# A routed-expert stage whose loop is skewed by one matrix, with another ending

## The reference, cut to what matters

```python
logits = t @ router_w + router_b            # t = rmsnorm(x) * norm_ffn_w, (320, 1024)
vals, idx = lax.top_k(logits, 4)            # 4 of 32 experts for each row
gates = jax.nn.softmax(vals, axis=-1)
for e in range(32):
    a = jnp.minimum(t @ w_gate[e] + b_gate[e], 7.0)
    u = jnp.clip(t @ w_up[e] + b_up[e], -7.0, 7.0)
    hid = (u + 1.0) * a * jax.nn.sigmoid(1.702 * a)
    y = y + combine[:, e:e + 1] * (hid @ w_down[e] + b_down[e])
x = x + y
y_prompt, y_sample = rmsnorm(x, final_norm_w)
```

## Time and profile before

| | |
|---|---|
| median of three executions | 1128.1 us (1128.0 to 1129.16) |
| the profiled execution, its own time | 1130.27 us |
| its span, first to last instruction | 1128.4 us |
| mean granted clock of TensorE | 0.994 |
| TensorE busy | 1103.0 us, 98% |
| VectorE / ScalarE / GpSimd busy | 394.5 / 162.7 / 18.2 us |
| DMA | 431.67 MB, mean 383 GB/s |
| chain that ended last | TensorE 79%, DMA 19%, VectorE 1% |

### The profile page before, as it was taken

The page is one execution under the profiler, slowest core; times in us unless marked ns, Lnnn a source line. Parts: engine busy times, 40 slices in busy tenths (PEclk is TensorE's granted clock), DMA queues, the critical chain, the costliest instruction groups (busy, mean ns, idle before and its releaser), DMA issues.

```text
span 1128.4 us, 15518 instructions
## 1 busy us (share of the span) xinstructions
PE 1103.0 (98%) x6341; PEld 454.0 (40%) x6341; DVE 394.5 (35%) x703; ACT 162.7 (14%) x284; POOL 18.2 (2%) x45
## 2 busy tenths in 40 slices
PE   8999999999999999999999999999999999999997
PEld 5657754433333333333333333333333333333333
DVE  4165385433333333333333333333333333233233
ACT  3100124211111111111111111111111111111102
POOL 0002000000000000000000000000000000000000
PEclk9999999999999999999999999999999999999997
DMA  9970247999999999999999999999999999999991
GB/s 323 333 227 22 129 159 298 396 428 427 436 428 430 432 432 433 429 432 433 432 430 432 432 432 432 431 432 432 433 431 431 432 433 429 429 429 428 427 423 63
DMA packets 41442, 431.67 MB, mean 383 GB/s; under 512 B 3809, under 2 KB 23069, under 8 KB 26431
## 3 DMA queue, kind: packets, MB, share of 16 engines
q1 hardware_dynamic: 40592, 430.38, 91.3%
q10 hardware_dynamic: 815, 0.82, 0.2%
HBM read 427.48 MB, written 3.71 MB: 382 GB/s over the span
## 4 chain that ended last, share of the span: by engine, by line
PE 79%; DMA 19%; DVE 1%; ACT 0%; issue 0%; SPq 0%; DVEq 0%
PE ps L1428 47%; DMA ring<-in_w_gate 15%; PE ps L1135 9%; PE ps L1402 5%; DMA ring<-in_w_up 4%; PE ps L1254 3%; PE ps L1319 3%; PE ps L1411 2%; PE ps L1322 1%; PE ps L1390 1%; PE ps L1471 1%; PE ps L1125 1%; PE ps L1384 1%; DMA x<-in_x_sample 0%; PE ps L1511 0%; PE ps L1513 0%
## 5 line engine op out<-in xcount | busy, mean ns | idle before, releaser
L1428 PE MATMUL ps<-ring,RT 128*64 128x512 f32 x3072 | 689.8, 594 | 11.7 <-DMA ring<-in_w_gate 10.3
L1428 PEld LDWEIGHTS ps<-ring,RT 128*64 128x64 f32 x3072 | 210.5, 137 | 410.3 <-issue 381.7
L985 DVE SCALAR_TENSOR_TENSOR x<-ps,gates,x 128x1024 f32<-128x1024 f32 (+1 forms) x93 | 102.9, 1106 | 127.6 <-PE ps L1402 126.5
L1135 PE MATMUL ps<-R,ring 128*128 128x320 f32 x384 | 107.5, 436 | 0.3 <-issue 0.3
L991 DVE TENSOR_TENSOR RT<-ps,R 128x512 f32<-128x512 f32 x32 | 22.1, 692 | 228.9 <-ACT R L632 228.9
L1135 PEld LDWEIGHTS ps<-R,ring 128*128 128x128 f32 x384 | 71.8, 190 | 31.2 <-issue 1.8
L1402 PE MATMUL ps<-R 64*128 64x512 bf16 x558 | 76.8, 381 | 0.0
L1025 DVE TENSOR_SCALAR RT<-ps 128x512 f32<-128x512 f32 x32 | 22.1, 692 | 143.1 <-PE ps L1428 143.1
L624 ACT ACTIVATE RT<-RT 128x512 f32<-128x512 f32 x32 | 20.2, 630 | 300.1 <-DVE RT L1019 300.1
L1402 PEld LDWEIGHTS ps<-R 64*128 64x128 bf16 x558 | 20.8, 98 | 86.0 <-issue 50.3
L603 ACT ACTIVATE RT<-ps 128x512 f32<-128x512 f32 x33 | 19.7, 597 | 237.1 <-PE ps L1322 237.1
(11 more groups left out here) (226 smaller groups left out, 559.2 us busy)
## 6 DMA issues: line engine op xcount, KB each, us to landing
ring<-in_w_gate SPq DMA_DIRECT2D x26, 4096.0 KB, 32.5
ring<-in_w_up SPq DMA_DIRECT2D x25, 4096.0 KB, 32.0
ring<-in_w_down SPq DMA_DIRECT2D x25, 4096.0 KB, 32.8
ring<-in_w_up SPq DMA_DIRECT2D x14, 2048.0 KB, 39.0
ring<-in_w_down SPq DMA_DIRECT2D x13, 2048.0 KB, 39.8
ring<-in_w_gate SPq DMA_DIRECT2D x12, 2048.0 KB, 40.8
ring<-in_w_in SPq DMA_DIRECT2D x14, 1024.0 KB, 12.7
ring<-in_w_out SPq DMA_DIRECT2D x4, 1024.0 KB, 10.0
```

The source lines that it names most:

```text
L985: STT(xb[b], rows, gates[:, par, b:b + 1], xb[b], ALU.mult, ALU.add).then_inc(accDone, 1)
L1135: ins = MM(ps[:, n % 2, 0:NT], slot_k(L, 256)[:, k, 128 * half:128 * half + 128], hT[:, k, :], start=(k == 0), stop=(k == KT - 1))
L1428: ins = MM(shape(ps[64 * half:64 * half + 64, bank, :]), lhs(k), cols(w, half), start=False, stop=(k == KT - 1))
```

## The change

1. **The loop is skewed.** TensorE now works gate and up of expert `j`, then down of expert `j - 1`. The matrices are loaded and used in the order g0 u0 g1 u1 d0 g2 u2 d1 ... g31 u31 d30 d31. The scatter put into the gate product of expert `j` is that of `j - 2`. `turn_gates` and `turn` of the next expert are put into the down product, after blocks 1 and 3. The transposes of the hidden activations stand between the down product and the next gate product. There are five buffers each of `eh`, `PT` and `gates` in place of three; `hidT` gets a place of its own.
2. **The last expert's rows are scattered as float32**: one copy of the product to SBUF (`yLast`), one float32 copy of the one-hot matrix (`PTLast`), 6 matmuls, no split.
3. **The final norm's weight comes by a transfer** that repeats it over the partitions, into a ring buffer that is free by then.
4. **The branch on rounds is turned**: `if rounds < 2: ending; else: further rounds, ending`.

```diff
+    I_GATE, I_UP, I_DOWN = [0] + [3 * j - 1 for j in range(1, E)], [1] + [3 * j for j in range(1, E)], [3 * j + 4 for j in range(E - 1)] + [MATS - 1]
@@ further_rounds
-            with eng.If(rounds > 1):
+            with eng.If(rounds < 2):
+                ending()
+                eng.nop()
+            with eng.Else():
                 close_round(0)
...
-                eng.nop()
-            with eng.Else():
+                ending()
                 eng.nop()
@@ sync engine
+            def outputs():
+
+                sp.wait_ge(wUsed, 4 * NEXT + START)
+                sp.dma_start(fnw[0], A["final_norm_w"].partition_broadcast(128)).then_inc(fnwIn, 16)
+                for half in range(2):
+                    w = A["final_norm_w"][HALF * half:HALF * half + HALF]
+                    sp.dma_start(fnw[2][64 * half:64 * half + 64], w.partition_broadcast(64)).then_inc(fnwIn, 16)
...
@@ ScalarE, one expert
+                        sigmoid(e)
+                        keep_rows(m, before)
+                        keep_slots(m, before * 3, buf(j + 1))
...
                         act.activation(ysb[0], ps[:, 2, :], ACT.Copy).then_inc(yHigh, 1)
-                        act.wait_ge(yRest, e + 1 + START)
+                        keep_hidden(e)
+                        act.wait_ge(yRest, before + 1 + START)
                         act.activation(ysb[1], yrest, ACT.Copy).then_inc(yMid, 1)
...
+                act.activation(PTLast[:], PT[buf(E - 1)], ACT.Copy).then_inc(ptLastOut, 1)
+                act.wait_ge(wUsed, (r + 1) * (LPE * E) + START)
+                act.wait_ge(xgTOut, p0 + (E + 1) + START)
+                act.activation(yLast, ps[:, 2, :], ACT.Copy).then_inc(yHigh, 1)
@@ TensorE
+                def gate_up(e, m, j, it, between=()):
+
+                    pe.wait_ge(ehDone, m + 1 + START)
+                    pe.wait_ge(xgTOut, m + 1 + START)
+                    pe.wait_ge(aDone, e + START)
+                    product(0, half_c(xgT), I_GATE[j], it, buf(j), between)
+                    pe.wait_ge(uDone, e + START)
+                    product(1, half_c(xgT), I_UP[j], it, buf(j))
+                    gather(m + 1)
+
+                def down(e, j, it, between):
+
+                    pe.wait_ge(yRest, e + START)
+                    product(2, half_c(hidT), I_DOWN[j], it, buf(j), between, operand=(hidTOut, e + 1 + START))
+
+                gate_up(e0, p0, 0, 0)
+                turn_hidden(e0)
+                turn_gates(p0 + 1)
+                turn(p0 + 1)
                 def experts(it, these):
 
                     for j in these:
...
+                        gate_up(e, m, j, it, [lambda: None] + [lambda b=b: scatter(b, e2, m2, buf(j - 2)) for b in range(3)] if j > 1 else [])
+                        down(before, j - 1, it, [lambda: turn_gates(after), lambda: turn(after)])
+                        turn_hidden(e)
...
+                down(e0 + (E - 1), E - 1, 0, [lambda b=b: scatter(b, e0 + (E - 2), p0 + (E - 2), buf(E - 2)) for b in range(3)])
+                pe.wait_ge(ptLastOut, r + 1)
+                pe.wait_ge(yHigh, e0 + E + START)
...
+                        ins = MM(to, PTLast[64 * half:64 * half + 64, t0:t0 + n], yLast[64 * half:64 * half + 64, :],
+                                 start=True, stop=True)
...
-            for part, ready in enumerate((yHigh, yMid, yLow)):
-                pe.wait_ge(ready, E + START)
-                for b, (t0, n) in enumerate(TOK):
...
-            for k in range(D // 128):
-                row = ident[0:FN + 8, FN + k:FN + k + 1]
-                at = 128 * (k % 4)
-                MM(ps[:, 4 + k // 4, at:at + 128], row.broadcast_to([FN + 8, 128]), parRows[:], start=True, stop=True)
-                half = slice(64 * (k // 4), 64 * (k // 4) + 64)
-                ins = MM(ps[half, 2, at:at + 128], row.broadcast_to([FN + 8, 64]), parRows[:], start=True, stop=True)
-            ins.then_inc(fnwMM, 1)
```

More of the change, by code:

```diff
@@ L404, in _ @@
+            further_rounds(sp, all_loads, ending=outputs)
             sp.wait_ge(yOut, 64)
@@ new lines, in norms @@
+            def norms():
+                bring_table(ACT.Sqrt, 3)
+                for b in range(3):
+                    act.wait_ge(accDone, 3 * (E - 1) + b + 1 + START)
+                    if b:
+                        act.wait_ge(finSq, b)
+                    act.activation(junk2[:, 0:WIDE[b]], xb[b], ACT.Square, accum_out=st[:, b:b + 1]).then_inc(finSq, 1)
+                    if b < 2:
+                        act.wait_ge(finSq, b + 1)
+                        total = st[:, b:b + 1]
+                    else:
+                        act.wait_ge(finFoldMM, 1)
+                        total = ps[:, 5, 0:1]
+                    act.activation(st[:, 3 + b:4 + b], total, ACT.Sqrt, bias=epsT[:], scale=1.0 / D).then_inc(finRoot, 1)
@@ L640, in _, with close_round @@
+            def close_round(r):
+                act.wait_ge(accDone, (r + 1) * (3 * E) + START)
+                act.sem_inc(aloneA, 1)
             one_round(0)
             act.wait_ge(roundsDone, 1)
[L642 to L655 removed]
+            further_rounds(act, one_round, close_round, ending=norms)
@@ L1029, in experts @@
-                        dve.wait_ge(accDone, e * 3 + 3 + START)
-                        keep_gates(m, col, buf(j + 1))
-                        gathered(m)
-                        split_rows(e)
-                experts(0, range(FIRST))
+                        rows = (p0 + (it * PER_LOOP + (j - 2)), e0 + (it * PER_LOOP + (j - 2)), buf(j - 2)) if j > 1 else ()
+                        gate_up(e, m, col, j, r * (LPE * E) + it * (LPE * PER_LOOP), rows)
+                        split_rows(e0 + (it * PER_LOOP + (j - 1)))
@@ L1055, in _, with scales @@
-            for b in range(3):
-                dve.wait_ge(lastMM, b + 1)
-                rows = ps[:, LAST[b]:LAST[b] + 2, :].rearrange("p a n -> p (a n)") if b < 2 else ps[:, LAST[b], :]
-                STT(xb[b], rows, gates[:, buf(E - 1), b:b + 1], xb[b], ALU.mult, ALU.add).then_inc(moeDone, 1)
-            dve.wait_ge(moeDone, 3)
-            dve.wait_ge(fnwMM, 1)
-            for b in range(3):
-                final_scale(b)
+            def scales():
+                dve.wait_ge(fnwIn, 48)
+                for b in range(3):
+                    dve.wait_ge(finRoot, b + 1)
+                    dve.reciprocal(st[:, 6 + b:7 + b], st[:, 3 + b:4 + b]).then_inc(finScale, 1)
+                    dve.wait_ge(finScale, b + 1)
+                    STT(yout[:, b, 0:WIDE[b]], xb[b], st[:, 6 + b:7 + b], fnw[b], ALU.mult, ALU.mult).then_inc(finDone, 1)
@@ L1065, in _ @@
+            further_rounds(dve, one_round, rounds=rounds[0], ending=scales)
         @block.tensor
@@ L1461, in experts @@
-                        pe.wait_ge(xgTOut, m + START)
-                        pe.wait_ge(aDone, e + START)
-                        product(0, 0, half_c(xgT), e, it, j, [lambda: None] + [lambda b=b: scatter_before(b) for b in range(3)]
-                                if not isinstance(e, int) or e > 0 else [])
-                        pe.wait_ge(uDone, e + START)
-                        product(1, 1, half_c(xgT), e, it, j)
-                        gather(m)
-                        pe.wait_ge(hidDone, e + 1 + START)
@@ L1469, in experts @@
-                        pe.wait_ge(hidTOut, e + START)
-                        for c in range(4):
-                            ins = TR(ps[:, 4, 128 * c:128 * c + 128], fourth(hid, c), ident)
-                        ins.then_inc(hidTMM, 1)
-                        turn_gates(m)
-                        turn(m)
-                        pe.wait_ge(yRest, e + START)
-                        product(2, 2, half_c(hidT), e, it, j, operand=(hidTOut, e + 1 + START))
-                experts(0, range(FIRST))
+                        e, m = e0 + (it * PER_LOOP + j), p0 + (it * PER_LOOP + j)
```

265 lines of the change are left out of this document (134 added, 131 removed).

## The result

| | before | changed |
|---|---|---|
| median | 1128.63 us (four executions) | 1169.93 us (1168.71 to 1171.02, four) |
| ratio | | 1.0363, 95% interval 1.0345 to 1.0381 |
| the profiled execution, its span | 1130.27, 1128.4 us | 1171.02, 1169.2 us |
| mean granted clock of TensorE | 0.994 | 0.981 |

The forecast was 1122.3 us (range 1120.3 to 1126.2). The time is 47.6 us above it, on the other side, and beyond every rival.

What follows compares the result with a forecast made beforehand. The prediction took the weight transfer stream as the bound, TensorE close behind with 11.7 us of slack. A 7.8 us shorter ending and a 2.0 us later last product gave -5.8 us: 1122.3 us, range 1120.3 to 1126.2.

Steps and rivals of the forecast that it cites:

- every rival: Mild TensorE bound 1126.9 us (0.12), slower TensorE 1131.9 (0.08), visible end jump 1124.5 (0.09), serial float32 halves 1123.2 (0.09), free skew 1121.3.
- the stream has no hole to fill: Weight transfers during the expert loop: said to run full from 226 us on, at 427 to 436 GB/s.
- nothing of its own: Turned branch ahead of the ending: no separate gain counted, since VectorE's 2 us were hidden behind L1511.
- The ending, -7.8: From the last product's end to the first scale's reciprocal: 5.2 us rather than 13.0, so 7.8 us shorter.
- The float32 halves: Last expert's scatter: two row-tile halves taken to run together, 0.86 us a pair; if not, +0.9 us, chance 0.09.
- The jump at the end, taken 0, bound +2.5: Jump over further rounds, now after the ending: taken as hidden behind output transfers, at most one fetch, 2.5 us.
- a sign against it: Kernel's end: more than 4 us between the last issue of y_sample and the end would show the prediction wrong.
- The skew, +0.39 us an expert: TensorE's expert loop: three more layout changes an expert, 0.39 us, 12.1 us over 31 experts; bounds 0 and 0.54.
- T0 + 2.0: End of the last product: 2.0 us later than 1108.3, by TensorE's limit of 1110.3 against the stream's 1109.3.
- 0.13 each: TensorE's expert loop: each change of the array's layout was priced at 0.13 us.
- The sum: Whole kernel: -7.8 + 2.0 = -5.8 us, profiled execution 1124.5 us, median 2.2 us lower at 1122.3 us.

Runs made afterwards that it cites:

- run 7: Kernel before with only the final norm's weight brought by a transfer: 1125.68 us, ratio 0.9973.
- run 4: Kernel before with the norm's weight by a transfer and the branch on rounds turned on TensorE, VectorE and ScalarE: 1125.73 us, ratio 0.9968.
- run 1: Changed kernel with 100 unused semaphore increments strewn among TensorE's first projections, ahead of its loop: 1125.47 us, ratio 0.9962.
- run 9: Changed kernel with 32 unused semaphore increments ahead of TensorE's loop: 1125.8 us (one run).
- run 5: Changed kernel with 40 unused semaphore increments ahead of TensorE's loop: 1125.1 us (one run).
- run 12: run 6 with `turn_gates` and `turn` in one place of the down product rather than two: 1123.8 us, ratio 0.9959 to the kernel before.
- run 6: Changed kernel with 100 semaphore increments ahead of TensorE's loop, TensorE's and SyncE's jump over further rounds again ahead of the ending: 1123.85 us, ratio 0.9953.

## Why the prediction was wrong

**The step that failed** is one that the prediction did not take: it priced the loop body's instructions and said that "the stream has no hole to fill", counted "nothing of its own" for the turned branch, and weighed fetched code only at the branch on rounds, once, with a bound of 2.5 us. It never asked what the loop's own return costs once the code ahead of it changes length. The row that would have asked stood in the page of before: 22 packets of 16 KB for a program of which 6341 matmuls and as many weight loads were executed, some 50 packets' worth, means that the loop was not fetched again in five returns, and that this is a state which can be lost. Its price was in no row of before; but a single fetch after a branch cost VectorE 2.53 us, so even one in each of five returns is 12.7 us, twice the forecast gain. The section of the Trainium skill that the prediction cites for the branch on rounds holds the room of 2048 instructions too, a few lines away, and a loop of 1614 with the next block comes near it; the prediction used only the sentence that it was looking for. No rival held this; the range ended 44 us short. The runs showed in its place five returns of 9.1 to 9.5 us more each, 44.5 us of the time, which a shift of the code takes away.

By its own terms:

- **The ending, -7.8.** Right: 7.6 (16.7 less 9.1), seen in the changed kernel itself. The transfer brought 4.4 of it (run 7, forecast 4.5). The float32 halves do run beside each other: first sum at T0 + 1.9.
- **The jump at the end, taken 0, bound +2.5.** Mis-sized. From the first issue of y_sample to the end it was 3.4 us before, and 5.6 in the changed kernel, 5.2 in run 4, 4.95 in run 1, 4.7 and 4.5 in runs 9 and 5: 1.1 to 2.2 more. From the last issue to the end of the changed kernel it is 4.5 us (1164.7 to 1169.2), which the prediction had named as a sign against it. The rule of the Trainium skill that the prediction cites for it, that the jump is paid, agrees with these figures. What the prediction missed is that instruction packets run beside the outputs' transfers, which then take longer (3.8 us for 2.7), so the outputs are no cover. Turned in TensorE, VectorE and ScalarE, the branch gave nothing (run 4 against run 7).
- **The skew, +0.39 us an expert.** Right: 28.13 less 27.75 is 0.38, without a wait. That layouts cost 0.08 rather than 0.13 each in run 12 leaves some of the 0.38 to something else, or says that its changes are not all alike.
- **T0 + 2.0.** 1110.5, 1109.7, 1110.2, 1108.9 and 1109.4 in the shifted forms (forecast 1110.3 by TensorE, 1109.3 by the stream): right within 1.4, and nearer the stream's figure. In runs 5, 6, 9 and 12 the chain goes through the landing of the last up matrix, at 1083.3 to 1084.5 (forecast 1083.9), so the stream and not TensorE was the later one.
- **The sum.** The shifted kernel's profiled execution took 1126.44 us against 1124.5: 0.2 from T0, 0.2 from the scales, 1.5 from the end. Its median lies 3.2 above the forecast, since the forecast took 2.2 us off for the way from the profiled execution to the median, and here that was 1.0. The skew alone wasn't run; skew and float32 scatter together add nothing that can be told to the transfer and the branch (run 1 against run 4, 1125.5 and 1125.7).

## What to carry to other kernels

Before a change that alters the length of code ahead of or inside a hardware loop, read the queue of instruction packets: if there are far fewer packets than executed instructions divided by 256, the loop lives on code that is kept, and a shift of its place can end that (here 160 instructions did, and 32 brought it back); when a change loses time in equal pieces at each return, with "issue" as the releaser, shift the code by fillers before looking for a fault in the change. Writing the loop out avoids this too, at the price of the stream. And of a jump that nobody waits for, ask what else it shares: here it was worse behind the outputs than ahead of an idle stretch, by 0.4 to 1.2 us.

## What the runs showed of the hardware that was not expected

- A TensorE loop of 1613 instructions (6.3 packets of 256) returns five times without a fetch at six places in the program (q8 carries no packet from 700 to 1050 us in any of the six), and with about nine packets a return at two, at 9.4 us a return in the changed kernel and 10.6 in the kernel before. Nine packets are the whole loop and more, not just one that doesn't fit.
- Behind the idle stretches of such a return (2.91 and 3.46 us) the granted clock is 0.50, and ten matmuls take 4.43 us rather than 2.1.
- In a full stream 28 more instruction packets of 16 KB (0.46 MB) took the place of 1.1 MB of weights.
- With instruction packets beside them the transfers of y_prompt took 3.4 to 3.8 us rather than 2.7 (one or two packets on q8 and two or three on q14), and 2.9 with two of q14 alone.
